# Selection rounds of two score tiles interleaved on VectorE, maxima ahead of index waits, first head rounded a slot sooner

## The chip, the cores and the metric

The kernel runs on one core of a Trainium2 chip. The metric is the device time of one execution in microseconds, the lower the better. Its engines are TensorE (PE, with its weight loads shown as PEld), VectorE (DVE), ScalarE (ACT), GpSimd (POOL, here a DMA queue) and SyncE (SP, the main DMA queue). Each has its own instruction stream and they meet only in semaphores.

## The reference, cut to what matters

The reference is a diffusion-like first block (grouped attention, neighbourhood attention, Fourier and convolution branches, a mixture of 16 experts) followed by a second block of two layers. Only the layers of the second block are touched. Each layer projects 512 tokens of width 1024, and runs retention, a sparse attention (DSA) and a dilated attention on the columns, then an MLP. The sparse attention picks, for each query, its 128 best keys by an index score:

```
logits = einsum('bqhd,bsd->bqhs', qib, k_idx)
score  = einsum('bqhs,bqh->bqs', relu(logits), wb)      # 8 index heads
score  = where(causal, score, -inf)
_, idx = top_k(score, 128)
... softmax over the selected keys only
```

## The kernel before, in words

Tokens lie in four tiles of 128 (partition = query). The score matrix of tile tt is `IX[tt]`, 128 rows by (tt+1)*128 keys, so 256 columns for the second tile (tt = 1), 384 for the third, 512 for the fourth. The first tile has only 128 keys and needs no selection. The selection of a tile is 16 rounds: `v.max` writes the 8 largest values of each row into `TOP`, and `v.match_replace` overwrites these 8 in `IX[tt]` by a marker (in the trace a MATCH_VALUE_LOAD and a MATCH_REPLACE8). 16 rounds mark 128 keys, and `selected` turns the marks into a mask. `link` gives an instruction a semaphore increment and lets VectorE wait for it; each max and each replacement is linked, as each reads what the one before it wrote. `v.sem_inc(sems["paused"], 1)` in front of each is a bare semaphore instruction.

The order of work on every engine is written out by hand. A layer of the second block goes so around the change:

- `index(count)` (L3259) adds one index head to a tile's score. ScalarE makes `F` = relu of the logits (`relu`, L2120) and VectorE multiplies it by the head's weight and accumulates (L3266, L3268). There are 24 steps n: 0 to 7 for the second tile, 8 to 15 for the third, 16 to 23 for the fourth. ScalarE may not overwrite `F` before VectorE is done (`ix_dve`), and TensorE makes two logits at a time (`index_pair`, L1444, shown at L1451) once ScalarE has read the ones before. In steps 8 and 14 to 23 one round of the second tile's selection follows the step (L3272).
- Then six weight units u = 0 to 5 of four slots j each follow, counted q = 4u + j = 0 to 23 (L3372 to L3403). TensorE multiplies (L875) with a retention step after each slot (`retention`, L1481): scores of a key tile (L1497), or values (L1510). VectorE, at the start of a unit up to u = 4, makes the low part of the rounded weights (`lo`, L2392, 2.3 us). In the slots it has `scaled` (L3322, frees a PSUM bank), `retained` (L3317, multiplies two score tiles of the retention by the decay, and TensorE's value step waits for it) and rounds of selection: `TOP_1` for the second tile, `TOP_2` for the third (slots 5 to 13), `TOP_3` for the fourth (slots 14 to 23). `SCORES_FIRST` names the slots in which `retained` comes ahead of the rounds.
- At the end of slot 23 VectorE runs `mixed_remainders(0, l)` (L2807, L2808), the low part of the first attention head's queries and keys. It needs `mixed_rounded(0, l)` (L1902, L1903), which ScalarE runs in slot j = 2 of the last unit, between the retention's outputs (L2225) and the copies of the projection out of PSUM (L1631, four per unit). `TINY` at L2243 loads the table of Exp ahead.
- TensorE's `mixed_attention` waits for all four PSUM banks (so for the last L1631) and for the first head's remainders (`head_lo`) and starts with `scores(0)` (L1196, L1197). VectorE follows with `top` (L2818), ScalarE with Exp (L1910). The selection masks of all tiles are needed from there on. All six pairs of heads follow from that start in a chain.
- SyncE loads the queries and keys of heads 4 and 5 once the last `retained` is done (`ret_d`, L572), and further heads once `head_lo` comes. GpSimd stores the last projection (`dv`) once ScalarE has copied it; the weights of the output projection are loaded after that store (`weights_in`, L583).

Of the kernel before, what the change touches and what calls it, by code (L numbers as in the profile page):

```python
# [43 lines left out]
TAKEN = -3.0e38  # L44
# [16 lines left out]
class Tally:  # L61
# [18 lines left out]
    def next(self, name, k=1):  # L80
        v = self.at(name, k)
        self.skip(name, k)
        return v
# [31 lines left out]
STORES_2 = [("sqk", 0, 4), ("sv", 1, NT), ("rv", 1, NT), ("rqk", 0, 4), ("dk", 2, 4), ("dq", 0, 4), ("dv", 1, NT)]  # L115
IXSLOTS = [(1, 3), (1, 3), (0, 2, 3), (1, 3), (0, 2, 3)]
TOP_1 = [1, 1, 1, 0]
TOP_2 = [0] * 5 + [1] + [2] * 6 + [1, 2] + [0] * 10
TOP_3 = [0] * 14 + [1, 1, 1, 2, 2, 2, 1, 2, 2, 2]
SCORES_FIRST = (4, 5, 6, 7, 14, 15, 16, 17)  # L120


# [8 lines left out]
def stored(seq, s, upto=None):  # L131

    n = 0
    for name, b, k in seq:
        n += 16 * k if b == s else 0
        if name == upto:
            break
    return n


def program(nc, t, out, turns, only_first=False):
    ctx = ExitStack()
    with ctx:
        def sb(name, shape, dt=F32):
            return ctx.enter_context(nc.sbuf_tensor(name, shape, dt))
# [9 lines left out]
        sems = Sems(nc, ctx)  # L155
# [38 lines left out]
        SM = sb("SM", [P, 4, 32])  # L194
        MXA, MXB, NM, DEN, RD = (sb(n, [P, 2]) for n in ("MXA", "MXB", "NM", "DEN", "RD"))
        TOP = sb("TOP", [P, 8])
        WIX = sb("WIX", [P, NT, 8])
        EID = sb("EID", [P, 8], I32)
        XROW, YROW = sb("XROW", [P, NTILE], I32), sb("YROW", [P, NTILE], I32)
# [98 lines left out]
        IX = [SEL[:, tt, 0:(tt + 1) * P] for tt in range(NT)]  # L298
# [1292 lines left out]
        def _(act):  # L1591
            T = Tally(act, turns, "act", {**{b: 1 for b in BANKS}, **{b: 2 for b in PAIRS}})
# [307 lines left out]
            def mixed_rounded(s, l):  # L1900
                act.wait_ge(sems[f"qk_landed{s}"], T.next(f"qk_landed{s}", 64))
                act.activation(QX[s ^ l], QS[s], ACT.Copy)  # L1902
                act.activation(KX[s ^ l][:, 0:S], KS[s][:, 0:S], ACT.Copy).then_inc(sems["head_hi"], 1)  # L1903
# [207 lines left out]
            def layer(l):  # L2111
# [24 lines left out]
                def latents_and_index():  # L2136
# [5 lines left out]
                    for j in range(4):  # L2142
                        out(j)
                        act.activation(TM[:, j, 0:448], BK[j][:, 0:448], ACT.Copy, scale=TOKEN[:, j:j + 1])
                        act.activation(TM[:, j, 448:512], BK[j][:, 384:448], ACT.Copy, scale=TOKEN[:, j:j + 1])
                        act.activation(WIX[:, j, :], BK[j][:, 448:456], ACT.Copy,
                                       scale=INDEX[:, j:j + 1]).then_inc(sems[BANKS[j]], 1)
# [73 lines left out]
                def retained(u, j):  # L2221
                    pair, kt, hd, tiles = retention_turn(u * 4 + j)
                    for tt in tiles:
                        act.wait_ge(sems["ret_o"], T.next("ret_o"))
                        act.activation(XN[:, tt, hd * HD:(hd + 1) * HD], OBR[tt % 2], ACT.Copy).then_inc(sems["ret_oe"], 1)  # L2225
# [13 lines left out]

                def first_head(j):  # L2240
                    retained(4, j)
                    if j == 2:
                        act.activation(TINY, IDN[:, 0:1], ACT.Exp)  # L2243
                        mixed_rounded(0, l)
                unit(copies(lambda j: ST[1][:, j, :], UN, 4, "st_filled1", first_head, TOKEN), False)
# [128 lines left out]
        def _(v):  # L2374
            T = Tally(v, turns, "dve", {**{b: 1 for b in BANKS}, **{b: 2 for b in PAIRS}})
# [4 lines left out]
            link_sem = "dve_self"  # L2380

            def link(ins):

                ins.then_inc(sems[link_sem], 1)
                v.wait_ge(sems[link_sem], T.next(link_sem))
# [10 lines left out]
            def unit(evac=None, more=True):  # L2396
                if more:
                    lo()
                if evac is not None:
                    evac()  # L2400
                T.skip("gemm_done:out", 4)
# [849 lines left out]
            def layer(l):  # L3251
# [7 lines left out]
                def index(count):  # L3259
                    for _ in range(count):  # L3260
                        n, tt, ih = next(at)
                        nk = (tt + 1) * P
                        v.wait_ge(sems["ix_act"], T.next("ix_act"))
                        w = WIX[:, tt, ih:ih + 1]
                        if ih == 0:
                            ins = v.tensor_scalar(IX[tt], F[:, n % 2, 0:nk], w, None, ALU.mult)  # L3266
                        else:
                            ins = v.scalar_tensor_tensor(IX[tt], F[:, n % 2, 0:nk], w, IX[tt], ALU.mult, ALU.add)  # L3268
                        ins.then_inc(sems["ix_dve"], 1)
                        v.wait_ge(sems["ix_dve"], T.next("ix_dve"))  # L3270
                        if n == 8 or n >= 14:
                            top_rounds(1, 1)  # L3272
                        if ih == 7:
                            link(v.tensor_tensor(IX[tt][:, nk - P:nk], IX[tt][:, nk - P:nk], CM[:], ALU.add))

                def top_rounds(tt, n):

                    for r in range(n):
                        v.sem_inc(sems["paused"], 1)
                        link(v.max(TOP[:], IX[tt]))  # L3280
                        v.sem_inc(sems["paused"], 1)
                        link(v.match_replace(IX[tt], TOP[:], IX[tt], TAKEN))  # L3282

                def selected(tt):

                    link(v.tensor_scalar(IX[tt], IX[tt], 0.5 * TAKEN, NEG, ALU.is_gt, ALU.mult))

                def rotated():
# [83 lines left out]
                for u in range(6):  # L3372
                    if u == 1:
                        retained(0)
                        top_rounds(1, 2)
                        selected(1)
                    unit(None, u < 5)
                    for j in range(4):
                        q = u * 4 + j
                        if q in SCORES_FIRST and q > 4:  # L3380
                            retained(q - 4)
                        if u == 0:
                            index(2 if j in IXSLOTS[4] else 0)
                            top_rounds(1, TOP_1[j])
                        top_rounds(2, TOP_2[q])
                        if q == 13:
                            selected(2)
                        top_rounds(3, TOP_3[q])
                        if q == 23:
                            mixed_remainders(0, l)  # L3390
                        if u in (1, 3):
                            scaled(STB[2] if u == 1 else ST[0][:], j)
                        if u and q not in SCORES_FIRST:
                            retained(q - 4)
                    if u == 0:
                        v.wait_ge(sems["row_in"], T.next("row_in"))
                    if u == 2:
                        v.wait_ge(sems["st_written0"], stored(STORES_1, 0) + l * stored(STORES_2, 0) + stored(STORES_2, 0, "rqk"))
                    if u in (1, 3):
                        v.wait_ge(sems[BANKS[3]], T.at(BANKS[3]))  # L3400
                        v.sem_inc(sems["st_filled2" if u == 1 else "st_filled0"], 1)
                    if u % 2:
                        skip_banks()  # L3403
# [60 lines left out]
                for g in range(NPAIR):  # L3464
                    last = g == NPAIR - 1
                    m, n = UPAIR * g, 7 * g
# [147 lines left out]
```

## Time and profile before

| what | value |
|---|---|
| median of 3 runs | 2703.71 us (2699.12 to 2706.64) |
| profiled execution | 2699.56 us, span 2697.5 us |
| mean granted TensorE clock | 0.969 |
| PE, DVE, ACT busy | 93%, 71%, 47% of the span |
| chain that ended last | PE 66%, DVE 15%, DMA 8%, ACT 6% |

The span is what the profile covers of one execution; 2.06 us of the profiled execution's own time lie outside it. The two layers of the second block lie at about 1344 to 2010 us and 2010 to 2697 us, and the stages named above at about 1414 to 1536 us and 2094 to 2216 us. A timeline row gives start and duration in us, engine, line, operation, operands and count, and in brackets how long the engine was idle ahead of it and what released it.

### The profile page before, as it was taken

What the parts mean: (1) busy time and instruction counts of PE and PEld (TensorE: products, weight loads), DVE (VectorE), ACT (ScalarE), POOL (GpSimd) and SP (SyncE); (2) the same over time, 40 slices, a digit from 0 to 9 for tenths busy, and PEclk for the clock granted to TensorE, in tenths of its full rate; (3) what the DMA queues carried; (4) which work ended last, traced back from release to release, by engine and by line L of the source; (5) the groups of instructions that cost most, each with busy time, mean ns of one, the idle gap of its engine ahead of it and who ended that gap; (6) DMA issues with size and microseconds to landing.
All of it is one profiled execution on the core that took longest, in us unless ns stands there. A gap on an engine that the chain in (4) does not pass through costs nothing.

```text
span 2697.5 us, 31361 instructions
## 1 busy us (share of the span) xinstructions
PE 2497.4 (93%) x11667; PEld 1962.2 (73%) x11667; DVE 1920.5 (71%) x2679; ACT 1281.3 (47%) x1773; POOL 153.5 (6%) x186
## 2 busy tenths in 40 slices
PE   5899999999996999999699889999999988999998
PEld 2776877677775788788576667888887665688886
DVE  5465566677856898899638875866773887586678
ACT  5432255555433777778433364433453326443343
POOL 0111000000000111121001000000000010000000
PEclk8999999999997999999899999999999999999999
DMA  6457535473532899999533432322323343322331
GB/s 226 166 181 251 168 104 135 118 166 113 192 141 73 332 372 375 358 353 356 168 100 125 135 104 86 109 95 94 125 66 102 109 131 114 100 92 96 110 125 39
DMA packets 229583, 431.86 MB, mean 160 GB/s; under 512 B 63381, under 2 KB 86436, under 8 KB 229443
## 3 DMA queue, kind: packets, MB, share of 16 engines
q1 hardware_dynamic: 211978, 386.83, 43.3%
q0 software_dynamic: 17232, 43.02, 4.7%
q8 instruction: 88, 1.44, 0.2%
q14 instruction: 53, 0.43, 0.1%
q10 hardware_dynamic: 232, 0.14, 0.0%
HBM read 399.00 MB, written 46.68 MB: 165 GB/s over the span
## 4 chain that ended last, share of the span: by engine, by line
PE 66%; DVE 15%; DMA 8%; ACT 6%; issue 4%; SPq 1%; POOL 0%; DVEq 0%; ACTq 0%; POOLq 0%
PE BKP L875 30%; PE BKP L1085 5%; PE SCP L910 2%; PE SCP L911 2%; PE SCP L908 2%; DMA W<-in_w_expert_gu_dram 2%; PE BKP L1215 2%; DVE WL L3162 2%; DMA G<-in_w_expert_gu_dram 2%; DVE G L3282 2%; PE BKP L1129 2%; DVE TOP L3280 2%; ACT WH L2047 2%; PE BKP L1408 1%; PE TPP L1116 1%
## 5 line engine op out<-in xcount | busy, mean ns | idle before, releaser
L875 PE MATMUL BKP<-hH,WH 128*128 128x512 f32 x736 | 293.2, 398 | 12.4 <-ACT Z L1661 2.7
L875 PE MATMUL BKP<-hL,WH 128*128 128x512 f32 x736 | 287.6, 391 | 0.0
L875 PE MATMUL BKP<-hH,WL 128*128 128x512 f32 x736 | 287.1, 390 | 0.0
L2392 DVE TENSOR_TENSOR WL<-W,WH 128x2048 fp32r<-128x2048 f32 x64 | 146.6, 2291 | 171.2 <-ACT WH L1602 168.8
L1602 ACT ACTIVATE WH<-W 128x2048 fp32r<-128x2048 f32 x64 | 122.5, 1914 | 218.9 <-PE BKP L875 155.5
L875 PE MATMUL BKP<-WH,hH 128*128 128x512 f32 (+2 forms) x448 | 178.0, 397 | 10.1 <-issue 3.8
L875 PEld LDWEIGHTS BKP<-hH,WH 128*128 128x128 f32 x736 | 138.6, 188 | 53.8 <-issue 15.4
L875 PE MATMUL BKP<-WH,hL 128*128 128x512 f32 (+2 forms) x448 | 172.1, 384 | 0.0
L875 PE MATMUL BKP<-WL,hH 128*128 128x512 f32 (+2 forms) x448 | 171.4, 383 | 0.0
L875 PEld LDWEIGHTS BKP<-hL,WH 128*128 128x128 f32 x736 | 138.5, 188 | 29.9
L875 PEld LDWEIGHTS BKP<-hH,WL 128*128 128x128 f32 x736 | 138.8, 189 | 27.3
L3162 DVE TENSOR_TENSOR WL<-G,WH 128x2048 fp32r<-128x2048 f32 x45 | 103.0, 2291 | 22.3 <-ACT WH L2047 22.1
L1408 PE MATMUL BKP<-WH,hH 128*128 128x512 f32 x276 | 113.1, 410 | 3.5 <-DVE hL L3169 2.1
L3162 DVE TENSOR_TENSOR WL<-W,WH 128x2048 fp32r<-128x2048 f32 x46 | 105.2, 2289 | 13.3 <-ACT WH L2047 13.0
L875 PEld LDWEIGHTS BKP<-WH,hH 128*128 128x128 f32 x448 | 85.9, 192 | 34.4 <-issue 16.3
L1411 PE MATMUL BKP<-WH,hL 128*128 128x512 f32 x276 | 108.7, 394 | 0.0
L1410 PE MATMUL BKP<-WL,hH 128*128 128x512 f32 x276 | 108.1, 392 | 0.0
L2047 ACT ACTIVATE WH<-G 128x2048 fp32r<-128x2048 f32 x45 | 86.3, 1918 | 41.4 <-DMA G<-in_w_expert_gu_dram 19.2
L2047 ACT ACTIVATE WH<-W 128x2048 fp32r<-128x2048 f32 x46 | 88.3, 1919 | 32.2 <-DMA W<-in_w_expert_gu_dram 21.3
L1085 PE MATMUL BKP<-hH,WL 128*128 128x512 f32 x256 | 102.1, 399 | 0.0
L875 PEld LDWEIGHTS BKP<-WH,hL 128*128 128x128 f32 x448 | 85.8, 191 | 16.5
L875 PEld LDWEIGHTS BKP<-WL,hH 128*128 128x128 f32 x448 | 86.1, 192 | 14.7 <-issue 0.5
(680 smaller groups left out, 6511.6 us busy)
## 6 DMA issues: line engine op xcount, KB each, us to landing
W<-in_w_expert_gu_dram SPq DMA_DIRECT2D x46, 1024.0 KB, 7.6
G<-in_w_expert_gu_dram SPq DMA_DIRECT2D x46, 1024.0 KB, 7.4
W<-in_w_in_dram SPq DMA_DIRECT2D x42, 1024.0 KB, 5.2
W<-in_w_expert_down_dram SPq DMA_DIRECT2D x24, 1024.0 KB, 6.6
G<-in_w_expert_down_dram SPq DMA_DIRECT2D x22, 1024.0 KB, 7.1
X<-in_w_mod_dram SPq DMA_DIRECT2D x16, 1024.0 KB, 7.5
X<-in_w_in_dram SPq DMA_DIRECT2D x16, 1024.0 KB, 8.6
W<-in_w_up_dram SPq DMA_DIRECT2D x16, 1024.0 KB, 5.5
```

Source lines behind the costliest of these rows:

```text
L875: mm = pe.matmul(BK[j][:, 0:cols], lt, rh, start=start and a == 0, stop=stop and a == len(q) - 1, skip_group_check=True)
L908: pe.matmul(bank, OPH[o][:, k, cols], WH3[s][:, k, :], start=opens and k == 0, stop=False, skip_group_check=True)
L910: pe.matmul(bank, OPH[o][:, k, cols], WL3[s][:, k, :], start=False, stop=False, skip_group_check=True)
L911: mm = pe.matmul(bank, OPL[o][:, k, cols], WH3[s][:, k, :], start=False, stop=k == UK - 1, skip_group_check=True)
L1085: mm = pe.matmul(BK[1][:, :], wp[:, k, j * P:(j + 1) * P], ap[:, k, :], start=k == 0 and a == 0, stop=k == NK - 1 and a == 2, skip_group_c ...
L1408: pe.matmul(dst, ah[:, k0 + kk, :], wh[:, kk, c], start=k0 + kk == 0, stop=False, skip_group_check=True)
L1410: pe.matmul(dst, ah[:, k0 + kk, :], wl[:, kk, c], start=False, stop=False, skip_group_check=True)
L1411: mm = pe.matmul(dst, al[:, k0 + kk, :], wh[:, kk, c], start=False, stop=k0 + kk == last, skip_group_check=True)
L1602: act.activation(WH[s][:], W[s][:] if raw is None else raw, ACT.Copy).then_inc(sems["w_hi"], 1)
L2047: act.activation(ring_h(m, s0), ring_w(m, s0), ACT.Copy).then_inc(sems["w_hi"], 1)
L2392: v.tensor_tensor(WL[s][:], W[s][:] if raw is None else raw, WH[s][:].bitcast(F32), ALU.subtract).then_inc(sems["w_lo"], 1)
L3162: v.tensor_tensor(ring_l(m, s0), ring_w(m, s0), ring_h(m, s0).bitcast(F32), ALU.subtract).then_inc(sems["w_lo"], 1)
```

## The change

The rounds of the third and the fourth tile run together: in a slot of `TOP_BOTH` one round of each, in the order max of the third, max of the fourth, replacement of the third, replacement of the fourth, each waiting only for the one before it on its own tile. The fourth tile gets its own buffer of maxima in `SM`. The rounds spread over slots 5 to 14, 16 to 19, 21 and 22. In the index steps 8 and 14 to 23 the second tile's max is issued ahead of the wait for `F`, and its replacement behind the step, so that one max and one index step stand between waits. `selected(2)` moves from slot 13 to slot 23. On ScalarE the table load and `mixed_rounded(0, l)` move from slot 2 to slot 1 of the last unit.

```diff
-TOP_2 = [0] * 5 + [1] + [2] * 6 + [1, 2] + [0] * 10
-TOP_3 = [0] * 14 + [1, 1, 1, 2, 2, 2, 1, 2, 2, 2]
+TOP_BOTH = [0] * 5 + [1] * 10 + [0, 1, 1, 1, 1, 0, 1, 1, 0]
@@
         TOP = sb("TOP", [P, 8])
+        TOPS = [TOP[:], SM[:, 2, 24:32]]
@@ first_head (ScalarE)
                     retained(4, j)
-                    if j == 2:
+                    if j == 1:
                         act.activation(TINY, IDN[:, 0:1], ACT.Exp)
                         mixed_rounded(0, l)
@@ index (VectorE)
                         nk = (tt + 1) * P
+                        selecting = n == 8 or n >= 14
+                        if selecting:
+                            v.sem_inc(sems["paused"], 1)
+                            v.max(TOP[:], IX[1]).then_inc(sems[link_sem], 1)
+                            maxima = T.next(link_sem)
                         v.wait_ge(sems["ix_act"], T.next("ix_act"))
...
                         ins.then_inc(sems["ix_dve"], 1)
+                        if selecting:
+                            v.wait_ge(sems[link_sem], maxima)
+                            v.sem_inc(sems["paused"], 1)
+                            link(v.match_replace(IX[1], TOP[:], IX[1], TAKEN))
                         v.wait_ge(sems["ix_dve"], T.next("ix_dve"))
-                        if n == 8 or n >= 14:
-                            top_rounds(1, 1)
@@
+                since = {2: 0, 3: 0}
+                def both_rounds(n):
+                    for r in range(n):
+                        for tt in (2, 3):
+                            if since[tt]:
+                                v.wait_ge(sems[link_sem], since[tt])
+                            v.sem_inc(sems["paused"], 1)
+                            v.max(TOPS[tt - 2], IX[tt]).then_inc(sems[link_sem], 1)
+                            since[tt] = T.next(link_sem)
+                        for tt in (2, 3):
+                            v.wait_ge(sems[link_sem], since[tt])
+                            v.sem_inc(sems["paused"], 1)
+                            v.match_replace(IX[tt], TOPS[tt - 2], IX[tt], TAKEN).then_inc(sems[link_sem], 1)
+                            since[tt] = T.next(link_sem)
@@ selected
+                    if tt > 1:
+                        v.wait_ge(sems[link_sem], since[tt])
@@ the slots
-                        top_rounds(2, TOP_2[q])
-                        if q == 13:
+                        both_rounds(TOP_BOTH[q])
+                        if q == 23:
                             selected(2)
-                        top_rounds(3, TOP_3[q])
-                        if q == 23:
                             mixed_remainders(0, l)
```

## Rows read from the trace of the kernel before

**Rows 1.** Page, part 4: chain that ended last, shares by engine.

```profile
PE 66%; DVE 15%; DMA 8%; ACT 6%; issue 4%; SPq 1%; POOL 0%; DVEq 0%; ACTq 0%; POOLq 0%
```

**Rows 2.** Timeline of PE, second layer, weight units and start of attention.

```profile
2155.19 0.78 PE L1510 MATMUL TPP<-VSB,G 128*128 128x64 f32 x6
...
2191.58 0.88 PE L1510 MATMUL TPP<-VSB,G 128*128 128x64 f32 x6 [0.35 <-DVE AT L3317]
...
2209.13 1.00 PE L1510 MATMUL TPP<-VSB,AT 128*128 128x64 f32 x8
2215.41 0.47 PE L1196 MATMUL SCP<-WH 128*128 128x128 f32 x1 [5.28 <-DVE WH L2808]
```

**Rows 3.** Timeline of PE, first layer, the same places and one index pair.

```profile
1419.73 0.92 PE L1451 MATMUL SCP<-Z,G 64*128 64x384 f32 x4 [0.58 <-ACT F L2126]
...
1473.91 0.88 PE L1510 MATMUL TPP<-VSB,G 128*128 128x64 f32 x6 [0.55 <-DVE AT L3317]
...
1511.48 0.88 PE L1510 MATMUL TPP<-VSB,G 128*128 128x64 f32 x6 [1.43 <-DVE AT L3317]
...
1535.29 0.47 PE L1196 MATMUL SCP<-WH 128*128 128x128 f32 x1 [5.27 <-DVE WH L2808]
```

**Rows 4.** Timeline of DVE, second layer, last rounds and first head's remainder.

```profile
2210.58 0.69 DVE L3280 MAX8 TOP<-G 128x8 f32<-128x512 f32 x1
2211.42 0.09 DVE L3282 MATCH_VALUE_LOAD G<-TOP,G 128x8 f32 x1
2211.50 0.68 DVE L3282 MATCH_REPLACE8 G<-TOP,G 128x512 f32<-128x512 f32 x1
2212.32 0.70 DVE L3280 MAX8 TOP<-G 128x8 f32<-128x512 f32 x1
...
2214.66 0.69 DVE L2808 TENSOR_TENSOR WH<-KS,WH 128x512 fp32r<-128x512 f32 x1
```

**Rows 5.** Timeline of DVE, second layer, retained tiles, a third-tile round, scaled.

```profile
2146.83 0.55 DVE L3317 TENSOR_TENSOR G<-TPP,ES 128x384 f32<-128x384 f32 x1
2147.30 0.55 DVE L3317 TENSOR_TENSOR AT<-TPP,ES 128x384 f32<-128x384 f32 x1
2147.76 0.55 DVE L3280 MAX8 TOP<-G 128x8 f32<-128x384 f32 x1
...
2148.53 0.54 DVE L3282 MATCH_REPLACE8 G<-TOP,G 128x384 f32<-128x384 f32 x1
2149.11 0.69 DVE L3322 TENSOR_TENSOR BIG<-BKP,BIG 128x512 f32<-128x512 f32 x1
...
2154.01 0.28 DVE L3317 TENSOR_TENSOR AT<-TPP,ES 128x128 f32<-128x128 f32 x1
...
2191.25 0.28 DVE L3317 TENSOR_TENSOR AT<-TPP,ES 128x128 f32<-128x128 f32 x1
```

**Rows 6.** Timeline of ACT, second layer, last weight unit.

```profile
2206.79 1.28 ACT L2243 ACT_TABLE_LOAD   x1
...
2208.72 0.61 ACT L1903 ACTIVATE WH<-KS 128x512 fp32r<-128x512 f32 x1
...
2210.34 0.68 ACT L1631 ACTIVATE ST<-BKP,MODP 128x512 f32<-128x512 f32 x1
...
2211.68 0.61 ACT L1903 ACTIVATE WH<-KS 128x512 fp32r<-128x512 f32 x1
```

**Rows 7.** Timeline of DVE, first layer, index steps 8 and 9.

```profile
1417.37 0.43 DVE L3280 MAX8 TOP<-G 128x8 f32<-128x256 f32 x1
...
1418.47 0.62 DVE L3268 SCALAR_TENSOR_TENSOR G<-F,WIX,G 128x384 f32<-128x384 f32 x1
```

**Rows 8.** DMA issues, 2185 to 2280 us: KB each, median us to landing.

```profile
KS<-kT_scratch SPq DMA_DIRECT2D x19, 128.0 KB, 3.1
...
v_scratch<-ST POOLq DMA_DIRECT2D x4, 256.0 KB, 4.6
```

**Rows 9.** Windows, first layer: stretch, length, busy times, granted clock, DMA.

```profile
1536.00:1548.00 12.00, 10.00 (x34) 5.68 (x35) 9.91 (x26) 6.81 (x21) 0.00 (x0) 0.73 0.99 280
```

## The prediction

> **What bounds the kernel now.** I read the chain of waits first. Over the whole span TensorE holds 66% of it and VectorE 15% [rows 1], so a change on VectorE alone pays only where VectorE ends last. The timeline of TensorE shows where that is: at the start of attention it idles 5.28 us in the second layer and 5.27 us in the first, released by the first head's remainder on VectorE (L2808) [rows 2, 3]. Smaller waits of the same kind stand at the retention's values (L1510): 0.55 and 1.43 us in the first layer, 0.35 us in the second, where the first of the two shows no wait [rows 2, 3]. One index pair waits 0.58 us for a relu [rows 3]. The reader is to see that the rest of the selection, over 60 us of VectorE's time per layer, is beside TensorE's work. What can be won is thus near 6 to 7 us a layer, whatever VectorE saves.
>
> **What the next limit is.** Behind the last product TensorE does its retention step at 2209.13, done at 2210.13. ScalarE copies the last PSUM bank at 2210.34, done at 2211.02, and TensorE needs that bank [rows 2, 6]. So scores can start at about 2211.1 and not before: of the wait that ends at 2215.41, 4.3 us can go and 1 us stays. In the first layer the wait is the same within 0.01 us, and so is the sum.
>
> **Cost of a round before.** Fourth tile: max at 2210.58, value load at 2211.42, replacement at 2211.50, next max at 2212.32 [rows 4]. That is 1.74 us, of which 0.84 - 0.69 = 0.15 us and 0.82 - 0.68 = 0.14 us are gaps behind the end of the op. Third tile: the max of 0.55 us at 2147.76, the replacement of 0.54 us at 2148.53 [rows 5], so 0.77 + 0.54 + 0.15 = 1.46 us. A round of each is 3.20 us. Where no bare semaphore instruction stands behind the wait, the gap is only 0.04 us (replacement done at 2149.07, L3322 at 2149.11 [rows 5]), so about 0.11 us of each gap is that instruction being run after the wait instead of beside work.
>
> **Cost of a pair of rounds after.** Where an op does not wait for the one in front, it starts ahead of that one's end: 384 columns of 0.55 us follow each other at 0.47 and 0.46 us, and the second of these successors is a max that has the bare semaphore instruction in front of it [rows 5]. I carry the same 0.09 us over to 512 columns: 0.60 us. Interleaved, each wait is for an op that ended at least 0.4 us earlier, so it is passed while the other tile's op runs. The pair is 0.47 + 0.60 for the maxima, 0.08 + 0.46 and 0.08 + 0.60 for value loads and replacements: 2.29 us. No row shows an op starting directly behind a max or a replacement with no wait between, so both ends: at best 2.29 us; if these two ops let nothing overlap, their durations with 0.08 us per value load, 0.55 + 0.69 + 0.62 + 0.76 = 2.62 us; and if the waits help nothing at all, 3.20 us. I take 2.29 us, the row nearest to it being the max that overlaps the op in front. Sixteen pairs save 16 x 0.91 = 14.6 us of VectorE's time per layer, three times what TensorE's wait can give back.
>
> **Where this time goes, slot by slot.** Unit 1 held 1 + 2 + 2 rounds of the third tile and now holds three pairs. The last `retained` ahead of the values has two slots of rounds in front of it: slot 5 grows from 1.35 us (2147.76 to 2149.11 [rows 5]) to 2.29, slot 6 shrinks from 1.46 + 1.35 = 2.81 us to 2.29. Together 0.4 us later. The second layer hides it: `retained` ended at 2154.29 and TensorE came at 2155.19 [rows 2, 5]. The first layer doesn't: 0.55 us becomes 0.95 us. Units 2 and 3 held 8 rounds of the third tile, then 3 and 2 of the fourth, and a mask of about 0.4 us: some 11.7 and 7.8 us by these round times. Now 4 and 3 pairs: 9.2 and 6.9 us. VectorE enters unit 4 some 3.5 us sooner, with its next low part waiting no more for VectorE itself, and makes the last `retained` about 2.6 us sooner than 2191.53 although a whole pair stands in front of it. The waits of 1.43 and 0.35 us [rows 2, 3] go. Behind it come 5 pairs, 11.5 us, then the mask of the third tile (0.4 us, now here) and VectorE stands idle by about 2201, 9 us ahead of the new limit. So TensorE's product stage ends 1.43 - 0.40 = 1.0 us sooner in the first layer and 0.35 us in the second, and the bank copy with it.
>
> **First head sooner on ScalarE.** Table load at 2206.79 to rounding done at 2209.33 is 2.54 us [rows 6]. It goes one slot forward, 3.5 us (distance of the slot 2 and slot 3 rows), to about 2203.3 to 2205.8. The copy of slot 1 is then 2.7 us later, at 2206.5, which nobody needs before the bank wait at 2211. The keys were loaded behind the last `retained` at 2191.53 [rows 5] with 3.1 us to landing [rows 8], nine queue entries of about 0.6 us at most, so they are there by 2201. With VectorE idle the remainder (1.4 us) is done near 2207.3. Left in slot 2 it would be done at 2210.7, still ahead of 2211.1: this edit is worth nothing by itself here, and costs nothing. It gives 3.4 us of margin.
>
> **Maxima ahead of the index waits.** In step 8 the max at 1417.37 to the next step at 1418.47 takes 1.10 us [rows 7]. Now the max (0.34 us start to start) is ahead, and value load, replacement and wait take about 0.08 + 0.41 + 0.04, with the step's own overlap: the next step comes about 0.48 us sooner. That step releases the relu for which TensorE waited 0.58 us [rows 3], so 0.5 us per layer goes. The other ten rounds save 4.5 us on a VectorE that idles anyway before the first decay product; no wait of TensorE names it there. Below nothing: step 8 itself is 0.34 us later, but its relu is not the one awaited.
>
> **After the start.** ScalarE rounds the second head until 2212.29 [rows 6] and its first Exp stands behind that. With TensorE 0.35 us sooner this is 2211.95 against an Exp at 2216.61, so it allows 4.7 us and no more. The rest of attention follows from its start. TensorE's clock was granted 0.73 in the first 12 us of it, after the idle time [rows 9]; that is between 1.2 and 2.4 GHz. A shorter idle may keep it up; since the chain there is mostly VectorE and ScalarE, I give it 0, at most 1 us a layer.
>
> **Sum.** First layer 4.3 + 1.0 + 0.5 = 5.8 us; second 4.3 + 0.35 + 0.5 = 5.15 us; together 11.0 us. The profiled execution of 2699.56 us would come to 2688.6. It lies 4.15 us under the median of 2703.71, whose three runs spread over 7.5 us, and I forecast the median: 2692.7 us. I take 0.3% (8.1 us) as the bound of what a measurement tells from no change.
>
> **Rivals.** *A, an op directly behind a max or replacement doesn't overlap:* pair 2.62 us. Speaking for it: a max gives out its result only at the end; against it: nothing measured. `retained` ahead of the values is 1.05 us later, unit 4's comes at 2192.2 instead of 2191.53. TensorE waits 0.7 us more in the second layer, 0.4 us more in the first. The gain is 4.3 - 0.7 + 4.3 - 0.4 + 1.0 = 8.5 us, time 2695.2.
>
> *B, waits cost nothing that interleaving could give back (pair 3.20 us):* the only mechanism that ends slower. Three pairs in unit 1 make `retained` 2.2 us later (waits of 1.4 and 2.8 us), and in unit 4 the last `retained` comes at about 2198.7, 7.2 us later, because 13 rounds of the fourth tile that lay behind it are spread ahead of it. TensorE then ends its products 7 us later: scores at 2218.2 instead of 2215.41, the first layer 2.4 us late, less 1.0 us for the index: 4 us slower, 2707.9. Between A and B the sign turns at a pair of 3.0 us. Against it stand the 0.47 us rows [rows 5].
>
> This rival has a page. The Trainium skill, "VectorE: DVE Perf Modes", section "The DRAIN you can't avoid", says that the next op does not start until the pipe is empty, that eight copies took the same time with a semaphore after each as with one after the last, and advises to reduce the number of ops, not of semaphores. By that rule the pair is B's, as the number of ops is unchanged. The trace disagrees: without a wait the starts lie 0.09 us nearer than the duration, with one 0.04 to 0.15 us farther [rows 4, 5].
>
> *C, the gain is given back inside attention:* the output weights wait for the store of the projection, whose four pieces land 4.6 us after issue [rows 8] and start where they did; so do head loads that now meet that store. If half of the gain at the start ends in such a wait, 5.5 us stay: 2698.2. Against it: these loads have some us of margin in the timeline. *D, larger:* the clock stays up, 2 us more, 2690.7.
>
> **How the numbers follow.** Forecast 0.55, A 0.17, C 0.12, B 0.08, D 0.08. Range: the forecast's median can lie 3 us off by the spread of the runs, D gives the low end, A and most of C the high end: 2687.5 to 2700. Faster by over 8.1 us: most of forecast and D, half of A, 0.68. Slower by as much: B with bad luck, 0.06. The rest, 0.26, is within.
>
> **What would show it.** Right: pairs start 2.3 us apart in the timeline of VectorE; TensorE's wait ahead of L1196 falls to about 1 us and names ScalarE's copy (L1631); the wait at 1511.48 is gone, that at 1473.91 is near 1 us; VectorE idles over 5 us in the last unit. Wrong: pairs of 2.6 us or more; L1196 still released by L2808; a wait for ST or KS loads inside attention that before has none.

## The result, and the profile after

The changed kernel takes 2685.7 us (median of 5 runs, 2684.43 to 2689.52) against a median of 2703.71 us (also of 5 runs) for the kernel before, a ratio of 0.9936 with a 95% interval of 0.9921 to 0.9951. That is 18 us less by the medians and 13 to 21 us by the interval; 11.0 us were forecast, and 2685.7 lies under the stated range. The profiled execution went from 2699.56 to 2684.43 us, its span from 2697.5 to 2682.4 us.

The page of the kernel after, part 4, the chain that ended last by engine:

```profile
PE 75%; DVE 11%; DMA 5%; ACT 5%; issue 3%; SPq 1%; POOL 0%; DVEq 0%; ACTq 0%; POOLq 0%
```

Against [rows 1] VectorE has lost 4 points of the chain and DMA 3. The DMA part was in no term of the prediction.

Timeline of TensorE, kernel after, the first index pair of each layer and the places of [rows 2, 3]:

```profile
1378.68 0.70 PE L1451 MATMUL SCP<-Z,G 64*128 64x256 f32 x4
1415.36 0.92 PE L1451 MATMUL SCP<-Z,G 64*128 64x384 f32 x4
1452.60 1.13 PE L1497 MATMUL SCP<-QSB,KS 64*128 64x512 f32 x4
1468.30 0.88 PE L1510 MATMUL TPP<-VSB,G 128*128 128x64 f32 x6 [0.84 <-DVE AT L3343]
1504.29 0.78 PE L1510 MATMUL TPP<-VSB,G 128*128 128x64 f32 x6
1523.88 0.30 PE L1196 MATMUL SCP<-WH 128*128 128x128 f32 x1 [1.15 <-ACT ST L1631]
2053.90 0.70 PE L1451 MATMUL SCP<-Z,G 64*128 64x256 f32 x4
2128.20 1.13 PE L1497 MATMUL SCP<-QSB,KS 64*128 64x512 f32 x4 [0.28 <-DMA ES<-in_k_decay_dram]
2143.87 0.88 PE L1510 MATMUL TPP<-VSB,G 128*128 128x64 f32 x6 [0.81 <-DVE AT L3343]
2199.44 0.30 PE L1196 MATMUL SCP<-WH 128*128 128x128 f32 x1 [1.15 <-ACT ST L1631]
```

The starts of attention wait 1.15 us for ScalarE's copy and not 5.27 and 5.28 us for the first head's remainder. The waits of 0.58, 1.43 and 0.35 us are gone, and the first L1510 of each layer waits 0.84 and 0.81 us. The forecast had all of this but the 0.81 us: it let the second layer hide the later `retained`. What it did not have at all is in four rows of the kernel before that the prediction had left out: the first index pair and the first decay score (L1497) of each layer.

```profile
1382.59 0.70 PE L1451 MATMUL SCP<-Z,G 64*128 64x256 f32 x4
1458.52 1.13 PE L1497 MATMUL SCP<-QSB,KS 64*128 64x512 f32 x4 [1.46 <-DMA ES<-in_k_decay_dram]
2062.24 0.70 PE L1451 MATMUL SCP<-Z,G 64*128 64x256 f32 x4
2138.95 1.17 PE L1497 MATMUL SCP<-QSB,KS 64*128 64x512 f32 x4 [2.25 <-DMA ES<-in_k_decay_dram]
```

TensorE waited there 1.46 and 2.25 us for the load of the decay table, and after the change for nothing and 0.28 us.

These rows cut a layer into three stretches that can be compared between executions: *index* (first L1451 to first L1497), *product* (first L1497 to the first L1196 of attention) and *rest* (that L1196 to the first L1451 of the next layer). "First index pair" is where the second block's first one stands. In us, each from the same rows of one profiled execution of each kernel; the kernels are those of the experiments below:

| kernel | index, layers 1 and 2 | product, 1 and 2 | rest | first index pair |
|---|---|---|---|---|
| before | 75.93, 76.71 | 76.77, 76.46 | 526.95 | 1382.59 |
| before_again | 75.56, 75.77 | 76.80, 76.47 | 527.76 | 1388.37 |
| quarter_load | 74.44, 75.30 | 77.35, 76.48 | 527.36 | 1383.60 |
| index_only | 73.90, 73.91 | 76.82, 76.50 | 528.51 | 1383.27 |
| pairs_only | 75.15, 75.92 | 71.24, 71.23 | 528.24 | 1384.80 |
| index_late | 74.98, 75.77 | 71.24, 71.24 | 526.39 | 1386.07 |
| index_early | 73.90, 73.91 | 71.29, 71.26 | 527.13 | 1382.80 |
| after | 73.92, 74.30 | 71.28, 71.24 | 530.02 | 1378.68 |
| after_again | 73.90, 74.24 | 71.28, 71.25 | 527.33 | 1379.01 |
| pairs_serial | 74.02, 73.92 | 81.21, 81.23 | 527.45 | 1384.08 |
| later_pairs | 73.90, 73.90 | 70.17, 70.17 | 527.10 | 1382.21 |
| copy_first | 73.95, 73.94 | 69.43, 69.42 | 527.70 | 1384.02 |

With the two executions of each kernel averaged, the product stretches gained 153.25 - 142.53 = 10.7 us for both layers (forecast 4.3 + 1.0 + 4.3 + 0.35 = 9.95), the index stretches 151.98 - 148.18 = 3.8 us (forecast 1.0). Together 14.5 us. The rest stretch scatters by 3.6 us between kernels whose code there is the same, and the first index pair by 10 us, behind a first block that no kernel changes. From the second layer's L1196 to the end of the span it is 482.0 to 483.4 us in the four kernels with the old rounds and 482.0 to 484.6 us in the eight others.

The interleaved rounds, timeline of VectorE, kernel after, one pair and the start of the next:

```profile
1473.44 0.55 DVE L3300 MAX8 TOP<-G 128x8 f32<-128x384 f32 x1
1473.91 0.68 DVE L3300 MAX8 SM<-G 128x8 f32<-128x512 f32 x1
1474.50 0.07 DVE L3305 MATCH_VALUE_LOAD G<-TOP,G 128x8 f32 x1
1474.56 0.54 DVE L3305 MATCH_REPLACE8 G<-TOP,G 128x384 f32<-128x384 f32 x1
1475.02 0.08 DVE L3305 MATCH_VALUE_LOAD G<-SM,G 128x8 f32 x1
1475.09 0.68 DVE L3305 MATCH_REPLACE8 G<-SM,G 128x512 f32<-128x512 f32 x1
1475.68 0.55 DVE L3300 MAX8 TOP<-G 128x8 f32<-128x384 f32 x1
```

A pair takes 2.24 us. The second max starts 0.47 us after a first one of 0.55 us, the next op 0.59 us after a max of 0.68 us.

The end of the product stage, VectorE of the kernel after, first layer:

```profile
1513.27 0.35 DVE L3312 TENSOR_SCALAR G<-G 128x384 f32<-128x384 f32 x1
1518.54 0.69 DVE L2807 TENSOR_TENSOR WH<-QSB,WH 64x512 fp32r<-64x512 f32 x1 [4.93 <-ACT WH L1903]
1519.24 0.69 DVE L2808 TENSOR_TENSOR WH<-KS,WH 128x512 fp32r<-128x512 f32 x1
1524.47 0.29 DVE L2818 CUSTOM_DVE_ANT_0 AT<-SCP,G 128x128 f32<-128x128 f32 x1 [4.20 <-PE SCP L1197]
```

VectorE idles 4.93 us ahead of the remainders and 4.20 us behind them; the remainders are done at 1519.9, 4 us ahead of TensorE's start.

### The profile page after: what moved, and what is told of

It reads as the page before. It is cut to its first block, busy times and chain, and to the rows that moved or that the text cites. A ratio compares the mean times of both kernels' runs of the same rounds, so it can differ in the third digit from the quotient of the medians.

```text
span 2682.4 us, 31335 instructions
## 1 busy us (share of the span) xinstructions
PE 2493.3 (93%) x11667; PEld 1959.3 (73%) x11667; DVE 1904.5 (71%) x2679; ACT 1281.8 (48%) x1773; POOL 150.6 (6%) x186
## 4 chain that ended last, share of the span: by engine, by line
PE 75%; DVE 11%; DMA 5%; ACT 5%; issue 3%; SPq 1%; POOL 0%; DVEq 0%; ACTq 0%; POOLq 0%
PE BKP L875 34%; PE BKP L1085 6%; PE SCP L910 2%; PE SCP L911 2%; PE SCP L908 2%; PE BKP L1408 2%; PE BKP L1411 2%; PE BKP L1410 2%; PE BKP L1215 2%; PE BKP L1129 2%; DVE WL L3162 2%; PE TPP L1116 1%; DMA W<-in_w_expert_gu_dram 1%; PE TPP L910 1%; PE TPP L908 1%
## 5 line engine op out<-in xcount | busy, mean ns | idle before, releaser
L2392 DVE TENSOR_TENSOR WL<-W,WH 128x2048 fp32r<-128x2048 f32 x64 | 146.6, 2291 | 170.6 <-ACT WH L1602 168.3
L875 PEld LDWEIGHTS BKP<-WL,hH 128*128 128x128 f32 x448 | 85.7, 191 | 14.9 <-issue 0.5
```

The source lines that it names most:

```text
L875: mm = pe.matmul(BK[j][:, 0:cols], lt, rh, start=start and a == 0, stop=stop and a == len(q) - 1, skip_group_check=True)
L2392: v.tensor_tensor(WL[s][:], W[s][:] if raw is None else raw, WH[s][:].bitcast(F32), ALU.subtract).then_inc(sems["w_lo"], 1)
```

## The experiments

**The two kernels once more, and the two halves of the change.** The first question was where 18 us come from when the stages named in the forecast hold 11. index_only is the kernel before with the new index steps alone. pairs_only is the changed kernel with the old index steps and the first head in slot 2:

```diff
-                    if j == 1:
+                    if j == 2:
                         act.activation(TINY, IDN[:, 0:1], ACT.Exp)
```

> The kernel before, unchanged, for a second trace of it. The profiled pair (before, after) differs by 3.9 us already where the second block begins (third projection block of TensorE at 1343.7 against 1339.8 us), in code that the change does not touch. Theory 'scatter': this difference is run to run, so this trace reaches the same instruction anywhere within some 4 us of 1343.7, and its time is within 0.3% of the kernel before. Rival 'program': the program before is slower there by itself; then this trace reaches it at 1343 to 1345 us again and every trace of the changed program at 1339 to 1340. Theory 'collision' (the waits of 1.46 and 2.25 us for the decay table, L1497, come from a 1 MB weight load that meets the store of queries and keys): both waits are there again.

> The changed kernel, unchanged. Scatter: ratio about 0.9945 (11 us by the steps forecast plus 4.8 us at the decay table, less 2 to 4 us given back in attention: 12 to 16 us), and the second block begins within 4 us of the other traces. Program: second block begins 3 to 4 us sooner than in the kernel before and the gain is 17 us or more. Collision: no wait over 0.4 us for the decay table in either layer.

> Of the change, only the second tile's maxima ahead of the index waits; rounds and first head as before. Collision: the low part ahead of the third weight unit is done 1.6 us sooner against TensorE, the 1 MB load issued after it ends before the store of queries and keys, the store lands in about 3 us instead of 4 to 5, and the waits for the decay table go: 0.5 + 1.5 us in the first layer, 0.5 + 1.9 + 1.2 us (clock) in the second, together 5 to 6 us faster. VectorE is as late as before at the start of attention (5.3 us waits stay). Rival (my prediction's step: the other index rounds save nothing): 1 us faster, waits for the decay table as before.

> Of the change, only the interleaved pairs and their slots; index rounds and first head (slot 2) as before. Collision: waits for the decay table stay at 1.5 and 2.3 us; the start of attention is 5.3 us sooner against the first retention scores in the first layer and 4.3 us in the second, so 9 to 10 us faster less what attention gives back (2 us): 7.5 us. The first head's move is worth 0: TensorE's wait ahead of L1196 is 1.1 to 1.2 us and names ScalarE's copy. Rival (head move needed): the wait stays over 2 us and names L2808, gain under 6 us.

| kernel | median us (runs) | ratio to before, 95% interval |
|---|---|---|
| before_again | 2703.82 (11) | 1.0004, 0.9995 to 1.0013 |
| index_only | 2699.4 (11) | 0.9987, 0.9976 to 0.9999 |
| pairs_only | 2692.43 (6) | 0.996, 0.9946 to 0.9973 |
| after_again | 2686.68 (5) | 0.9945, 0.9932 to 0.9958 |

As ratios of 2703.4 us the halves bring 3.5 and 10.8 us, together 14.3, and the whole 14.9. They add up, and agree with the stretches: index_only gains (75.75 - 73.90) + (76.24 - 73.91) = 4.2 us in the index stretches, pairs_only 10.8 us in the product stretches. pairs_only starts attention with the same 1.15 us wait for L1631 and has the same product stretches as the whole change (71.24 us against 71.28), so the earlier first head is worth nothing here, as forecast.

Three expectations were off. index_only was to be 5 to 6 us faster and is 3.5 to 4.2, pairs_only was to be 7.5 us faster and is 10.8, and before_again was to reach the second block within some 4 us of the first trace: its first index pair there comes 5.8 us later.

The missing piece is the wait at L1497. It goes with the index edit. With the pairs alone it stays, though in the first layer 0.61 us is shorter than the 1.46 and 1.08 us of the two executions of the kernel before; no run shows why. index_only:

```profile
1457.17 1.13 PE L1497 MATMUL SCP<-QSB,KS 64*128 64x512 f32 x4
2136.41 1.13 PE L1497 MATMUL SCP<-QSB,KS 64*128 64x512 f32 x4
```

pairs_only:

```profile
1459.95 1.13 PE L1497 MATMUL SCP<-QSB,KS 64*128 64x512 f32 x4 [0.61 <-DMA ES<-in_k_decay_dram]
2135.35 1.13 PE L1497 MATMUL SCP<-QSB,KS 64*128 64x512 f32 x4 [1.44 <-DMA ES<-in_k_decay_dram]
```

**Which index steps, and why.** The decay table is loaded by SyncE in one group with the retention's queries and keys, and this group waits until GpSimd's store of the rotated queries and keys (`rqk`, L761) has landed. In the kernel before the group is late because the store is slow. SyncE's 1 MB weight load (L376), released by a low part (L2392) on VectorE, runs beside it. Kernel before, first layer, SyncE:

```profile
1442.70 0.37 SPq L376 DMA_DIRECT2D W<-in_w_in_dram  x1
1450.48 0.53 SPq L383 DMA_DIRECT2D QSB<-qT_scratch  x1
```

Kernel before, GpSimd:

```profile
1444.51 1.10 POOL L761 DMA_DIRECT2D qT_scratch<-ST  x2 [4.54 <-ACTq L2198]
```

Kernel before, DMA issues of the stretch 1434 to 1460 us (KB each, median us from issue to landing):

```profile
qT_scratch<-ST POOLq DMA_DIRECT2D x2, 256.0 KB, 4.0
kT_scratch<-ST POOLq DMA_DIRECT2D x2, 256.0 KB, 4.1
```

Kernel after, the timeline of SyncE and then of GpSimd:

```profile
1436.67 0.37 SPq L376 DMA_DIRECT2D W<-in_w_in_dram  x1
1445.01 0.53 SPq L383 DMA_DIRECT2D QSB<-qT_scratch  x1
```

```profile
1440.12 1.10 POOL L761 DMA_DIRECT2D qT_scratch<-ST  x2 [4.53 <-ACTq L2198]
```

There the store lands in 2.5 (queries) and 3.0 us (keys). The weight load is issued 3.45 us ahead of the store instead of 1.81 us, and the loads come 4.89 us behind the store's issue instead of 5.97. The index steps 14 to 17 stand in front of that low part, so two kernels split the new form between steps; the steps that `selecting` leaves out keep the old form:

```diff
-                        selecting = n == 8 or n >= 14
+                        selecting = n == 8 or 14 <= n < 18    # index_early
+                        selecting = n >= 18                   # index_late
```

A third, quarter_load, is the kernel before with no instruction of VectorE changed. Its weight load brings a quarter of the block (0.25 MB) and leaves out the rest:

```diff
-                blk(w2, 1992)
+                unit(w2[0:UN, bass.ds(1992, UN)])
...
+                sp.dma_start(W[s][:, 0:1, 0:UN], w2[UN:UN + P, bass.ds(1992, UN)]...
```

> The changed kernel, but the new form of the index step (maxima ahead of the wait) is kept only in the steps n = 8 and 14 to 17; steps 18 to 23 have the old form. The low part (L2392) whose end lets SyncE issue the 1 MB weight load lies behind step 17. Theory 'collision' (that load meets the store of the rotated queries and keys, and is earlier only because of the steps in front of its low part): everything that the whole index edit brings is here, so qT/kT land in 2.5 and 3.0 us in the first layer, the wait for the decay table (L1497) is under 0.3 us in both layers, first index pair to L1497 is 73.9 and 74.3 us, median 2685 to 2689. Rival 'VectorE's load' (the waits go because VectorE as a whole is ahead, so the six late steps count as well, 2.7 of the 4.5 us saved): the wait stays at over 0.5 us and the median is 2689 to 2693.

> The changed kernel, but the new form of the index step only in the steps 18 to 23; n = 8 and 14 to 17 have the old form. Collision: the steps in front of the low part are as before, so the weight load is issued as late as before against the store; qT/kT land in 4.0 and 4.2 us, L1497 waits 0.6 to 1.5 us for the decay table in both layers, L1451 waits 0.58 us: as the kernel with the pairs alone, 2691 to 2694. Rival 'VectorE's load': over half of the index gain is here, wait under 0.5 us, median 2687 to 2690.

> The kernel before, in which one weight load per layer of the second block (the last one ahead of the retention's loads, 1 MB) brings only its first quarter, 0.25 MB; the rest of that weight block is left out. No VectorE instruction is changed. Collision: with the load gone in about 1.3 us, the store of qT/kT lands in 2.5 to 3.1 us instead of 4.0 to 5.0, SyncE's retention loads are issued over 1 us sooner, and the wait at L1497 falls from 1.1 to 2.2 us to under 0.4 us in both layers, while L1451 still waits 0.58 us: median 2.5 to 3.5 us under the kernel before, ratio about 0.9989. Rival 'VectorE's load' (the store's landing is no matter of the load beside it): landing and waits unchanged, ratio 1.000.

index_early: 2685.46 us (6 runs), ratio 0.9942 (0.9928 to 0.9955). index_late: 2689.76 us (6 runs), 0.9958 (0.9942 to 0.9974). quarter_load: 2700.41 us (12 runs), 0.9995 (0.9984 to 1.0007). The intervals of the first two overlap, so their traces decide. L1497 in index_early:

```profile
1456.70 1.13 PE L1497 MATMUL SCP<-QSB,KS 64*128 64x512 f32 x4
2129.03 1.13 PE L1497 MATMUL SCP<-QSB,KS 64*128 64x512 f32 x4
```

In index_late:

```profile
1461.05 1.13 PE L1497 MATMUL SCP<-QSB,KS 64*128 64x512 f32 x4 [0.48 <-DMA ES<-in_k_decay_dram]
2134.45 1.13 PE L1497 MATMUL SCP<-QSB,KS 64*128 64x512 f32 x4 [1.33 <-DMA ES<-in_k_decay_dram]
```

In quarter_load, whose lines behind the edit are numbered 5 higher:

```profile
1458.04 1.13 PE L1502 MATMUL SCP<-QSB,KS 64*128 64x512 f32 x4
2138.05 1.13 PE L1502 MATMUL SCP<-QSB,KS 64*128 64x512 f32 x4 [0.80 <-DMA ES<-in_k_decay_dram]
```

and its DMA issues in 1434 to 1460 us:

```profile
qT_scratch<-ST POOLq DMA_DIRECT2D x2, 256.0 KB, 2.5
kT_scratch<-ST POOLq DMA_DIRECT2D x2, 256.0 KB, 3.0
```

Read by how far the weight load is ahead of the store in the first layer, and how long after the store's issue SyncE's first retention load goes out:

| kernel | load ahead of store, us | store issue to retention load: layers 1, 2 |
|---|---|---|
| before, before_again | 1.81, 1.80 | 5.97 and 5.99; 7.52 and 7.38 |
| pairs_only, index_late | 1.82, 1.80 | 6.20 and 5.92; 6.81 and 7.28 |
| index_only, index_early, after | 3.44, 3.45, 3.45 | 4.90, 4.90, 4.89; 5.63, 5.29, 5.52 |
| quarter_load | 1.80 | 4.89; 6.25 |

In the first layer this settles it: the steps in front of the low part carry the whole gain, and making the load small does the same to the store as moving it does. Against the rival, that VectorE's load as such counts, stands index_late: it takes waits off VectorE in six steps, but its waits at L1497 stay, its stores land as late as before (3.9 and 4.1 us in the first layer), and its index stretches are 0.3 us shorter than those of pairs_only where the whole edit brings 2.9 us. Its other numbers alone would not have decided: the first layer's 0.48 us and the median of 2689.76 us lie in the ranges that I had set for the rival, not in those of the theory. In the second layer quarter_load gives back only part, 0.80 us of wait remain where the index kernels have none to 0.28. I had expected under 0.4 us there. The store of the keys landed there in 3.9 us, against 5.1 us before and 3.3 to 3.6 us in the kernels with the new steps in front of the low part, so a smaller load does less there than an earlier one; why is open. Nor could quarter_load's median show it: of its 1.3 us in the first layer 0.57 us go again at L1510, since VectorE's `retained` did not come sooner (product 77.35 us against 76.80).

**Overlap or placing.** pairs_serial keeps slots and order of the changed kernel and waits for each max and each replacement before the next:

```diff
-                            v.max(TOPS[tt - 2], IX[tt]).then_inc(sems[link_sem], 1)
-                            since[tt] = T.next(link_sem)
+                            link(v.max(TOPS[tt - 2], IX[tt]))
+                            since[tt] = T.at(link_sem, 0)
```

and likewise at the replacement.

> The changed kernel, same slots and same order of the two tiles' rounds, but VectorE waits for each max and each replacement before it issues the next (as the rounds before the change did). Theory 'overlap' (the gain of the pairs is that no wait stands directly behind the op it waits for): a pair takes 3.0 to 3.2 us instead of 2.24, the first L1510 of a layer waits 2.5 to 3 us instead of 0.84, the last retained of the product stage is late as well, and the first decay product to the start of attention takes 78 to 80 us a layer instead of 71.3: slower than the kernel before by up to 5 us once the 4 us of the index edit are counted against it, median 2700 to 2708. Rival 'placing' (the gain comes from the new distribution of the rounds over the slots, and waits cost next to nothing): a pair takes about 2.4 us and the stage stays within 1 us of 71.3, median 2685 to 2688.

2708.9 us (12 runs), ratio 1.0019 (1.001 to 1.0028): slower than before, with the index edit still in it. VectorE of pairs_serial, one pair and the start of the next:

```profile
1485.05 0.56 DVE L3300 MAX8 TOP<-G 128x8 f32<-128x384 f32 x1 [0.17 <-DVE G L3305]
1485.79 0.69 DVE L3300 MAX8 SM<-G 128x8 f32<-128x512 f32 x1 [0.18 <-DVE TOP L3300]
1486.66 0.09 DVE L3305 MATCH_VALUE_LOAD G<-TOP,G 128x8 f32 x1 [0.17 <-DVE SM L3300]
1488.39 0.56 DVE L3300 MAX8 TOP<-G 128x8 f32<-128x384 f32 x1 [0.17 <-DVE G L3305]
```

A pair takes 3.34 us instead of 2.24 with the same instructions. TensorE of pairs_serial:

```profile
1475.64 1.54 PE L1510 MATMUL TPP<-VSB,G 128*128 128x64 f32 x6 [2.69 <-DVE AT L3343]
1518.05 0.88 PE L1510 MATMUL TPP<-VSB,G 128*128 128x64 f32 x6 [3.25 <-DVE AT L3343]
```

The product stretch is 81.2 us, 10 us longer than after and 4.4 to 4.8 us longer than before. The pair, the stretch and the median are all somewhat above what was expected (3.0 to 3.2 us, 78 to 80 us, at most 2708 us). Part of it is TensorE's clock, which fell with these waits. Windows of TensorE right behind the two waits, first layer (stretch, length, busy TensorE, granted clock, DMA share, GB/s; 0.50 is the level of 1.2 GHz, 0.67 a mean between it and 2.4 GHz):

```profile
1475.60:1482.20 6.60, 6.56 (x19) 0.50 0.14 52
1518.00:1523.10 5.10, 5.05 (x18) 0.67 0.60 184
```

From L1510 to the next value step TensorE took 6.56 and 5.12 us there, against 3.54 and 3.44 us in the changed kernel. The first of these losses is hidden: from 1470 to 1518 us VectorE has no idle time but its gaps, and its last `retained` sets the second wait, whose L1510 comes 59.95 us behind the first L1497, 7.0 us later than before. The second, 1.7 us, adds to the stretch. So the overlap is the whole gain of the pairs: without it, spreading the fourth tile's rounds early is a loss, some 1.7 us of it by the clock.

**Can more be had.** later_pairs takes the two pairs of slots 5 and 6 away from the first L1510 of a layer; copy_first adds to it that ScalarE's last copy goes ahead of the last retention output.

```diff
-TOP_BOTH = [0] * 5 + [1] * 10 + [0, 1, 1, 1, 1, 0, 1, 1, 0]
+TOP_BOTH = [0] * 7 + [1] * 8 + [0, 1, 1, 1, 1, 1, 1, 1, 1]
@@ copies (ScalarE), copy_first only
-                        if each:
+                        late = j == 3 and last_after
+                        if each and not late:
                             each(j)
                         act.activation(dst(j), BK[j][:, 0:cols], ACT.Copy, ...
+                        if each and late:
+                            each(j)
```

> The changed kernel with the pairs of rounds two slots later: none in slots 5 and 6, one in each of 7 to 14 and 16 to 23. Theory 'a pair ahead of the last retained of unit 1 costs its excess over the old rounds': with no round there the waits of 0.84 and 0.81 us at the first L1510 of a layer go to 0 (before they were 0.55), the last pair ends near 1518 in the first layer, still ahead of the first head's remainder, and the start of attention still waits 1.15 us for L1631: 1.6 us faster than the changed kernel, median 2684 to 2685.5. Rival: VectorE's last pairs now stand in front of the mixed remainder and delay the start of attention: L1196 waits over 1.5 us and names L2808, median 2687 or more.

> The kernel with the pairs two slots later, and in the last slot of the last unit ScalarE copies the PSUM bank of the projection (L1631) ahead of the last output of the retention (L2225), so that the copy no longer stands behind TensorE's last value step. Theory (the start of attention is now bound by this copy, as the 1.15 us wait names it): the copy starts about 0.95 us sooner, L1196 waits 0.2 to 0.3 us, first decay product to start of attention goes from 70.17 to 69.2 us in both layers; 1.9 us in all if attention carries it on, median 2680 to 2683. Rival (something else is due at the same time, the first head's remainder or the PSUM bank of the values): the wait stays over 0.8 us with another name, 70.0 us or more, no gain.

later_pairs: 2682.23 us (6 runs), ratio 0.9936 (0.992 to 0.9952). copy_first: 2685.91 us (5 runs), 0.9937 (0.9924 to 0.9949). Neither interval parts from that of the changed kernel. The traces do: 71.28 to 70.17 us of product stretch a layer, then 69.43. In later_pairs no L1510 waits any more. The start of attention in later_pairs and in copy_first, in that order (lines in copy_first are numbered 3 higher, so L2228 is the retention output L2225):

```profile
1526.28 0.30 PE L1196 MATMUL SCP<-WH 128*128 128x128 f32 x1 [1.15 <-ACT ST L1631]
```

```profile
1527.40 0.30 PE L1196 MATMUL SCP<-WH 128*128 128x128 f32 x1 [0.41 <-ACT BIG L2228]
```

later_pairs gained 1.1 us a layer where 0.8 was expected, because the wait cost more than its row: from the retention step ahead of it to the step behind it the changed kernel took 4.28 + 3.54 us with the wait of 0.84 us, and later_pairs 3.28 + 3.44 us without. copy_first gained 0.74 of the 0.95 us that its expectation named (its median lies above the 2680 to 2683 us expected), and then the output that it had moved behind the copy is what TensorE waits for. Together 3.7 us that the traces show in the two layers and the medians cannot.

## Why the prediction was too small

**Cost of a pair: right.** 2.24 us against 2.29. The overlap carried over from ordinary ops holds for max and replacement too. Rival A (2.62) is out. pairs_serial is rival B made real, at 3.34 us and not 3.20, since each of the four gaps is 0.17 us. The rival priced the product stage 2.4 (first layer) and 2.8 us (second) over the one before, measured were 4.4 and 4.8; less the 3.8 us of the index edit that is 5.4 us slower than before, and the medians say 5.7. Its sign was right, and so was its path to the last `retained` (7.2 us later forecast, 7.0 measured); the clock behind the wait, 1.7 us in the first layer, was in no term of it.

The Trainium skill, "VectorE: DVE Perf Modes", section "The DRAIN you can't avoid", reports that a semaphore after each of eight copies cost nothing over one after the last. Here VectorE ran as many instructions in pairs_serial as in the changed kernel (2679), and a wait directly behind each op cost 1.10 us a pair. The prediction left out a sentence of that section, that a next op that is not held starts earlier, and the trace agrees: ops of 0.55 us start 0.47 us apart. So the page as a whole did not speak for rival B as the prediction says.

**Start of attention: right.** 4.12 us a layer against 4.3, with the named releaser.

**Values: the waits nearly right, their worth too low.** Of the product stretches' gain 1.4 us in the first layer and 1.1 us in the second are not the start of attention; 1.0 and 0.35 us were forecast. In the first layer the first wait was to be 0.95 us and is 0.84, and the one of 1.43 us went. The sum took each wait at its row; a wait at L1510 lengthens the stretch by some 0.25 us more, as later_pairs shows, and one of two is gone. In the second layer I took the 0.35 us wait of [rows 2] as what could be won. In before_again it was 1.12 us and the stretch the same 76.47 us. In the profiled execution TensorE had run its products at 0.63 instead of 0.40 us after the 2.25 us wait, with this granted clock (length, busy TensorE, clock, DMA share, GB/s of the window 2138 to 2143 us, kernel before; 0.69 of full speed is a mean between the levels of 1.2 and 2.4 GHz):

```profile
2138.00:2143.00 5.00, 4.05 (x11) 0.69 0.17 36
```

That had moved the wait, not removed it: VectorE set the length of the stretch. The product stretch gained 5.2 us there for 4.65 forecast.

**Index steps: the step that failed.** I wrote that the ten other rounds save 4.5 us "on a VectorE that idles anyway before the first decay product; no wait of TensorE names it there". TensorE's wait there named a DMA, and so I took it for no matter of VectorE. VectorE's low part releases the weight load, the load shares its time with the store, the store's landing releases the loads of queries, keys and decay table, and TensorE waits for those. Without the 0.58 us of the index pair, that chain was worth 75.75 - 73.91 - 0.58 = 1.3 us in the first layer and 1.4 to 1.8 us in the second (index stretch of 76.24 against 74.27 or 73.91). All index stretches together gained 3.8 to 4.2 us against 1.0 forecast. The 0.5 us of the index pair itself was right (its wait of 0.58 us is gone).

Against the sum of 11.0 us the stretches thus hold 2.8 us more by the index steps, 1.1 us more by the values and 0.4 us less by the start of attention.

**Give-back in attention (C) and clock (D): not seen.** The rest stretch of the changed kernel was 530.02 us in one execution and 527.33 in the other, with 526.95 and 527.76 before. What looks like 3 us given back in the first trace is scatter, and the stretch behind the second start of attention shows no difference beyond its own scatter either. Nor did the shorter idle time keep the clock up. Windows of TensorE over the first 12 us of attention, first layer, kernel before and then after:

```profile
1535.29:1547.29 12.00, 10.00 (x33) 0.70 0.97 264
1523.88:1535.88 12.00, 9.48 (x34) 0.72 0.75 225
```

In the second layer it is 0.59 and 0.57.

**What stays open.** The stretches hold 14.5 us, the two comparisons 17.3 (13 to 21) and 14.9 us (11 to 18). Taken off the median of 2703.71 us, 14.5 us give 2689.2, which lies inside the stated range; the last 3.5 us down to 2685.7 are explained by no stretch that the change touches. Whether the first block, whose code is the same, is sooner in the changed kernel is not settled: its two executions reach the first index pair at 1378.7 and 1379.0 us, the ten others between 1382.2 and 1388.4, and kernels that differ from it in a few instructions lie among the ten.

## What to carry to other kernels

When an op on one engine moves, follow what it releases through the DMA queues: a TensorE wait that names a DMA can belong to a VectorE instruction some 16 us upstream, by way of a load that collides with a store. Where one engine runs two dependent chains, try to interleave them so that no wait stands directly behind the op it waits for (here 2.24 us a pair of rounds instead of 3.34), and check it with one version that waits serially. To size a wait, compare the whole stretch between two marks in several executions, not a single wait row.

## What the runs showed of the hardware

- First layer: two 256 KB stores of queries and two of keys land in 2.5 and 3.0 us (median) when the 1 MB load beside them started 3.45 us earlier or is a quarter as large, and in 3.9 to 4.0 and 4.1 to 4.3 us when it started 1.8 us earlier.
- A wait on an op directly ahead, with a bare semaphore instruction behind it, leaves 0.17 us of idle VectorE, and the overlap of some 0.09 us with the op ahead is lost as well: (3.34 - 2.24) / 4 = 0.27 us an op.
- After one wait of 2.25 us at L1497 TensorE ran some products at 0.63 us (granted clock 0.69 over 5 us); after those of 0.48 to 1.46 us at the same place they stayed at 0.40 us. Behind waits of 2.69 and 3.25 us at L1510 the granted clock was 0.50 over 6.6 us and 0.67 over 5.1 us.
- A wait of 0.84 us at L1510 cost 1.10 us between the steps on either side of it.
